# Order of the projection's side work and start of the recurrent stage in a fused two-block kernel

## The chip, the cores and the metric

The kernel runs on one core of a Trainium2 chip. The metric is the device time of one execution in microseconds; for the kernel before it is 2198.66 us, the median of three runs (2197.02 to 2201.4). TensorE is called PE, VectorE DVE, ScalarE ACT, GpSimd POOL and SyncE SP, as in the profile.

## The reference, cut to what matters

Two blocks work on one sequence of 512 tokens of width 1024. The first block normalises the tokens, projects them, and feeds 3072 of the projected columns (queries, keys, values; 8 heads of 128 each) through a convolution over 5 tokens and SiLU. Queries and keys are then scaled to unit length, and a gated delta rule runs over the tokens in both directions. The rest (a dilated attention, gates, a feed-forward part, and a second block of two hybrid layers) is not touched here.

```python
qkv = conv_over_5_tokens(proj[..., C_QA:C_ZA], conv_w)
qkv = jax.nn.silu(qkv)
qa = _l2norm(q heads) * (GDN_HEAD_DIM ** -0.5)
ka = _l2norm(k heads)
g_f = _gdn_decay(...)            # log-decay of each token and head
o_a = (_chunk_gated_delta(qa, ka, va, g_f, beta_f)
       + flip(_chunk_gated_delta(flip(qa), flip(ka), flip(va), flip(g_b), flip(beta_b))))
# recurrence: S_t = exp(g_t)(I - b_t k_t k_t^T) S_{t-1} + b_t k_t v_t^T,  o_t = S_t^T q_t
```

## The kernel before, in words

Every engine has its own program, written by hand; a helper notes for each instruction the semaphore value that it reaches, and the others wait for labels. An engine runs its program strictly in order. Results of PE go to one of 8 PSUM banks, which `job` (L365) hands out in rotation: a job waits until the job eight before it has been freed by its reader.

The **projection stage** ("qkv") makes 24 tiles of 128 columns by 512 tokens, numbered n and called (c, i): c from 0 to 5 (0, 1 queries, 2, 3 keys, 4, 5 values), i from 0 to 3. For each tile:

- PE multiplies it out, 24 matmuls (`fm`, L384, recorded on L396).
- ACT copies it from its bank (L831, here "the copy"). After the copies of i = 1 and 3 it also rounds a later piece of weights into its high part (`ahead`, L354), from which POOL makes the low part (L2152); both are 128x2048. It then finishes the tile before: SiLU (L819) once the convolution is done, and for c below 4 the square (L824).
- DVE convolves it: one operation on L863 and four on L866, all 128x512. Two buffers hold the copies and two the convolved tiles, so that the copy of tile n waits for the convolution of n-2.

Once in each c from 1 to 4 there is a **round of scaling** for c-1: PE sums the squares of its four tiles (`sums`, L763), ACT makes four reciprocal roots (`rsq`: four Ln, L800, then four Exp, L804), and DVE multiplies the four tiles by them (`scale_tiles`, L885). PE and ACT do this at i = 1, DVE at i = 2, after the convolution of that tile. Keys and values are also turned to token-major by PE (`turn`, L771) and copied out by ACT (`trans`, L810); values turn from a buffer of four tiles, which c = 5 writes again.

The log-decays are summed once: `gates_sum_pe` (L650) needs the label "g" of DVE (L724); ACT's `decays_act` and DVE's `gates_sums` and `gates_scales` go with it.

The **recurrent stage** ("gdn") works on four groups (direction, half of the heads), with 4 steps of 20 phases each, lagging by 0, 1, 8 and 9 slots:

```python
        PHASES = 20
        LAG = (0, 1, 8, 9)
        def in_flight():
            for slot in range(TT * PHASES + max(LAG)):
                for gi, (d, hf) in enumerate(groups):
                    if 0 <= slot - LAG[gi] < TT * PHASES:
                        s, ph = divmod(slot - LAG[gi], PHASES)
```

Phase 0 is PE's spread of the decays and ACT's shift (L996), phase 1 POOL's mask (L1035), phase 2 ACT's Exp (L1000), phase 3 the products qk and kk (L940) and DVE's two steps (L1073, L1076), phase 4 PE's transpose (L948) and DVE's first inverse (L1083, L1086); levels of matmuls follow. The values are first read in phase 17. `stage("gdn")` makes each of the four engines wait until PE, ACT and DVE have all ended the projection stage.

Of the kernel before, what the change touches and what calls it, by code (L numbers as in the profile page):

```python
# [15 lines left out]
ALU = mybir.AluOpType  # L16
ACT = mybir.ActivationFunctionType
# [152 lines left out]
def build(nc, xT, cols, base, gdnc, tabs, wgate, relb, sel, small, wts, out, scratch, old):  # L170
# [6 lines left out]
    with ctx:  # L177
# [553 lines left out]
        def gates_sums(dve, V):  # L731
            dve.wait_ge(*at(("pe", "gc")))
            V.tensor_copy(GCUM, ps("gc")[:, 0:64].rearrange("p (t c) -> p t c", c=16)).then_inc(*dve.did())
            V.tensor_copy(SM[5], ps("gc")[:, 64:128].rearrange("p (t c) -> p t c", c=16)).then_inc(*dve.did("gcc", free="gc"))
            dve.wait_ge(*dve.last())
            V.tensor_tensor(SM[4], SM[5], GCUM, ALU.subtract).then_inc(*dve.did("kd"))
            V.tensor_scalar(NEGC, GCUM, -1.0, None, ALU.mult).then_inc(*dve.did())

        def gates_scales(dve, V):
            dve.wait_ge(*at("eg"))  # L740
# [13 lines left out]
        def qkv_pe():  # L754
            pe = q["pe"]
            pe.stage("qkv", barrier=False)

            def sums(c):
                for i in range(4):
                    n = ("ss", c, i)  # L760
                    b = job(n)
                    pe.wait_ge(*at(("sq", c, i)))
                    pe.eng.matmul(b[:, :], ones, SQ2[:, i, :], start=True, stop=True).then_inc(*pe.did(("pe", n)))  # L763

            def turn(c):
                for i in range(4):
                    n = ("tr", c, i)
                    b = job(n)
                    pe.wait_ge(*at(("ktile", c, i) if c < 4 else ("vtile", c, i)))
                    for t in range(TT):  # L770
                        mm = pe.eng.transpose(b[:, t * P:(t + 1) * P], dst_tile(c, i)[:, t * P:(t + 1) * P], ident)  # L771
                    mm.then_inc(*pe.did(("pe", n)))

            for c in range(6):
                for i in range(4):
                    fm(("qkv", c, i), f"A{c}", i * P, HTS)
                    if c == 0 and i == 1:
                        gates_turn_pe()
                    if c == 1 and i == 0:
                        gates_sum_pe()  # L780
                    if 1 <= c <= 4 and i == 1:
                        sums(c - 1)
                    if c == 4 and i == 2:
                        turn(2)
                    if c == 5 and i == 0:
                        turn(3)
                    if c == 5 and i == 1:
                        turn(4)
            turn(5)

        def qkv_act():
            act = q["act"]
            act.stage("qkv")

            def rsq(c):
                for i in range(4):
                    act.wait_ge(*at(("pe", ("ss", c, i))))
                    if c:
                        act.wait_ge(*at(("scaled", c - 1, i)))
                    act.eng.activation(RS2[:, i, :], ps(("ss", c, i))[:, :], ACT.Ln, bias=col("eps"))\  # L800
                        .then_inc(*act.did(free=("ss", c, i)))
                act.wait_ge(*act.last())
                for i in range(4):
                    act.eng.activation(RS2[:, i, :], RS2[:, i, :], ACT.Exp, scale=-0.5).then_inc(*act.did(("rs", c, i)))  # L804

            def trans(c):
                dst = KTOK if c < 4 else VTOK
                for i in range(4):
                    act.wait_ge(*at(("pe", ("tr", c, i))))
                    act.eng.activation(dst[:, :, (c % 2) * 4 + i, :], ps(("tr", c, i))[:, :].rearrange("p (t c) -> p t c", c=P),  # L810
                                       ACT.Copy).then_inc(*act.did(free=("tr", c, i)))

            def finish(n):

                c, i = tiles[n]
                act.wait_ge(*at(("conv", n)))
                if c == 5:
                    act.wait_ge(*at(("pe", ("tr", 4, i))))
                act.eng.activation(dst_tile(c, i), CV[:, n % 2, :], ACT.Silu).then_inc(*act.did(("si", c, i), *([("vtile", c, i)] if c >= 4 else [])))  # L819
                if c < 4:  # L820
                    act.wait_ge(*act.last())
                    if c:
                        act.wait_ge(*at(("pe", ("ss", c - 1, i))))
                    act.eng.activation(SQ2[:, i, :], dst_tile(c, i), ACT.Square).then_inc(*act.did(("sq", c, i)))  # L824

            for n, (c, i) in enumerate(tiles):
                act.wait_ge(*at(("pe", ("qkv", c, i))))
                act.wait_ge(*at("xpzero"))
                if n >= 2:
                    act.wait_ge(*at(("conv", n - 2)))  # L830
                act.eng.activation(XP[:, n % 2, 2:S + 2], ps(("qkv", c, i))[:, :], ACT.Copy)\  # L831
                    .then_inc(*act.did(("xp", n), free=("qkv", c, i)))
                if i % 2:
                    ahead(f"A{c}", (i - 1) * P)
                if n:
                    finish(n - 1)
                if n == 1:
                    gates_act()
                if n == 5:
                    decays_act()  # L840
                if i == 1 and 1 <= c <= 4:
                    rsq(c - 1)
                if c == 4 and i == 3:
                    trans(2)
                if c == 5 and i == 0:
                    trans(3)
            finish(len(tiles) - 1)
            trans(4)
            trans(5)

        def qkv_dve():
            dve = q["dve"]
# [4 lines left out]
            for n, (c, i) in enumerate(tiles):  # L857
                dve.wait_ge(*at(("xp", n)))
                if n >= 2:
                    dve.wait_ge(*at(("si", *tiles[n - 2])))  # L860
                wc = lambda j: col("conv", (c * 4 + i) * CONV + j)
                cv = CV[:, n % 2, :]
                V.tensor_scalar(cv, XP[:, n % 2, 0:S], wc(0), None, ALU.mult).then_inc(*dve.did())  # L863
                for j in range(1, CONV):
                    dve.wait_ge(*dve.last())
                    V.scalar_tensor_tensor(out=cv, in0=XP[:, n % 2, j:j + S], scalar=wc(j), in1=cv, op0=ALU.mult,  # L866
                                           op1=ALU.add).then_inc(*dve.did(*([("conv", n)] if j == CONV - 1 else [])))
                if n == 1:
                    gates_biased(dve, V)
                elif n == 2:  # L870
                    gates_decay(dve, V)
                elif n == 4:
                    gates_sums(dve, V)
                elif n == 5:
                    gates_scales(dve, V)
                if 1 <= c <= 4 and i == 2:
                    scale_tiles(c - 1)

        def scale_tiles(c):
# [42 lines left out]

            return (ph - 5) // 2 + 1, (ph - 5) % 2

        def gdn_pe():
            pe = q["pe"]
            E = pe.eng
            pe.stage("gdn")

            def four(nm, s, gi, product, n=P, labels=()):  # L930

# [5 lines left out]
            for s, ph, gi, d, hf, c, k0 in in_flight():  # L937
# [3 lines left out]
                if ph == 0:  # L941
                    four("gr", s, gi, lambda o, h: mul(o, Gg[:, c, k0 + h:k0 + h + 1].broadcast_to([P, P]), tri(d)))
                elif ph == 3:
                    four("qk", s, gi, lambda o, h: mul(o, KF[:, 4 * hf + h, tok], QF[:, 4 * hf + h, tok]))
                    four("kk", s, gi, lambda o, h: mul(o, KF[:, 4 * hf + h, tok], KF[:, 4 * hf + h, tok]))
                elif ph == 4:
                    pe.wait_ge(*at(("abar", s, gi)))
                    four("p0", s, gi, lambda o, h: E.transpose(o, g[A_][:, h, :], ident))  # L948
# [21 lines left out]
                elif ph == 17:  # L970
                    if s:
                        pe.wait_ge(*at(("r", s, gi)))
                    pe.wait_ge(*at(("t", s, gi, 6)))
                    four("x", s, gi, lambda o, h: mul(o, g[U_][:, h, :], g[T_][:, h, :] if s else VTOK[:, c, 4 * hf + h, :]))
                elif ph == 19:
                    if s < TT - 1:
# [4 lines left out]
                    if s:  # L981
                        four("qs", s, gi, lambda o, h: mul(o, QF[:, 4 * hf + h, tok], ST[:, gi, h, :]))

        def gdn_act():
            act = q["act"]
            A = act.eng
            act.stage("gdn")
            for s, ph, gi, d, hf, c, k0 in in_flight():
                g = WRKG[gi]
                if ph == 0:  # L990
# [7 lines left out]
                elif ph == 2:  # L998
                    act.wait_ge(*at(("ddm", s, gi)))
                    A.activation(g[A_], g[A_], ACT.Exp).then_inc(*act.did(("gam", s, gi)))  # L1000
                elif ph in LEVELS and level(ph)[0] > 1 and not level(ph)[1]:

                    l = level(ph)[0] - 1
# [1080 lines left out]
        def _(eng):  # L2084
            q["pe"] = Queue(eng, "pe")
            load_pe()
            qkv_pe()
            gdn_pe()
            zg_pe()
            dil_pe()  # L2090
            merge_pe()
# [11 lines left out]
        def _(eng):  # L2103
            q["act"] = act = Queue(eng, "act")
            load_act()
            qkv_act()
            gdn_act()
            zg_act()
            dil_act()
            merge_act()  # L2110
# [170 lines left out]
```

## Time and profile before

| | |
|---|---|
| median of 3 runs | 2198.66 us |
| profiled execution, its own time | 2193.11 us |
| its span, first to last instruction | 2191.3 us |
| mean granted PE clock | 0.973 |
| busy share: PE / DVE / ACT / POOL | 95% / 45% / 34% / 28% |
| projection stage on PE | 35.75 to 209.5 us |
| recurrent stage on PE, first matmul | 211.03 us |

The span lies 1.8 us below the time of the same execution, and that time 5.6 us below the median of the runs. "Idle before" in a row is the time the engine stood still before the row, with what released it. Bars in a timeline merge like instructions that follow each other; the count stands after x.

### The profile page before, as it was taken

To read this page: it belongs to the slowest core of one execution; us is meant where nothing else is said; L and a number is where in the kernel's file an instruction comes from. 1 tells how busy PE (TensorE), PEld (TensorE's weight loads), DVE (VectorE), ACT (ScalarE), POOL (GpSimd) and SP (SyncE) were. 2 spreads that over 40 slices of the span, in tenths; PEclk is the share of its full clock that TensorE was granted. 3 is DMA by queue.
4 is the path that set the end of the run, shared out by engine and by line. 5 is a ranking of instruction groups with operands and counts; after the bars stand their busy time and mean duration, and the time that the engine had idled before them with its cause. 6 is when DMAs were issued, how large, how long until landed. Compare 5 with 4: busy or idle time off the path is not lost.

```text
span 2191.3 us, 27107 instructions
## 1 busy us (share of the span) xinstructions
PE 2082.2 (95%) x11564; PEld 1723.9 (79%) x11564; DVE 990.3 (45%) x1805; ACT 749.2 (34%) x1231; POOL 614.3 (28%) x206
## 2 busy tenths in 40 slices
PE   6998999999999999999889999988999999999998
PEld 3777999999977877787768888876686778776676
DVE  4895556565412222122376025133527753624762
ACT  4675132221533233222332122223324433334441
POOL 2331222133323223244325444422420004321001
PEclk9999899999999999999989999999999999999998
DMA  4221000000342233222212222222220003211001
GB/s 164 71 83 39 1 1 2 1 1 1 132 151 84 85 105 102 74 99 97 77 58 96 96 96 96 96 78 107 75 75 3 1 20 108 77 58 39 1 1 39
DMA packets 29009, 142.12 MB, mean 65 GB/s; under 512 B 2871, under 2 KB 7351, under 8 KB 14808
## 3 DMA queue, kind: packets, MB, share of 16 engines
q1 hardware_dynamic: 18944, 123.27, 15.8%
q10 hardware_dynamic: 9944, 17.12, 2.3%
q8 instruction: 91, 1.49, 0.3%
q14 instruction: 30, 0.25, 0.0%
HBM read 135.13 MB, written 5.24 MB: 64 GB/s over the span
## 4 chain that ended last, share of the span: by engine, by line
PE 88%; DVE 6%; ACT 4%; issue 1%; POOL 1%; DMA 0%; SPq 0%; POOLq 0%; DVEq 0%; ACTq 0%
PE bank L396 44%; PE bank L940 12%; PE bank L407 7%; PE bank L1778 5%; PE bank L1796 4%; PE bank L1785 3%; PE bank L597 2%; DVE WK L866 2%; PE bank L955 2%; PE bank L1273 1%; DVE WK L885 1%; ACT w_part L354 1%; PE bank L1249 1%; PE bank L1725 1%; PE bank L1243 1%
## 5 line engine op out<-in xcount | busy, mean ns | idle before, releaser
L396 PE MATMUL bank<-x_part,w_part 128*128 128x512 f32 x2976 | 699.3, 395 | 21.3 <-POOL w_part L2152 18.3
L396 PEld LDWEIGHTS bank<-x_part,w_part 128*128 128x128 f32 x2976 | 562.6, 190 | 143.7 <-POOL w_part L2152 18.7
L2152 POOL TENSOR_TENSOR w_part<-RAW,w_part 128x2048 fp32r<-128x2048 f32 (+1 forms) x90 | 402.9, 4480 | 815.3 <-ACT w_part L354 815.3
L940 PE MATMUL bank<-WK 128*128 128x64 f32 (+1 forms) x2336 | 281.1, 277 | 3.5 <-DVE WK L1086 1.7
L940 PEld LDWEIGHTS bank<-WK 128*128 128x128 f32 x2336 | 275.8, 196 | 4.3 <-DVE WK L1086 1.9
L2152 POOL TENSOR_TENSOR w_part<-WK,w_part 128x2048 fp32r<-128x2048 f32 (+1 forms) x30 | 126.2, 4205 | 386.0 <-ACT w_part L354 386.0
L354 ACT ACTIVATE w_part<-RAW 128x2048 fp32r<-128x2048 f32 (+1 forms) x90 | 166.3, 1849 | 179.4 <-PE bank L396 138.3
L396 PE MATMUL bank<-f_part,w_part 128*128 128x512 f32 x768 | 174.4, 389 | 0.0
L396 PEld LDWEIGHTS bank<-f_part,w_part 128*128 128x128 f32 x768 | 144.2, 188 | 29.9
L407 PE MATMUL bank<-w_part,x_part 128*128 128x256 f32 x1344 | 164.4, 284 | 0.0
L407 PEld LDWEIGHTS bank<-w_part,x_part 128*128 128x128 f32 x1344 | 162.1, 192 | 2.1 <-issue 1.5
L1778 PE MATMUL bank<-WK 64*128 64x512 f32 (+3 forms) x256 | 129.0, 589 | 5.5 <-ACT WK L1873 5.5
L1796 PE MATMUL bank<-WK 128*128 128x64 f32 x880 | 112.4, 268 | 0.0
L1796 PEld LDWEIGHTS bank<-WK 128*128 128x128 f32 x880 | 108.3, 192 | 0.2
L1785 PEld LDWEIGHTS bank<-BASE,WK 128*128 128x128 f32 x440 | 48.5, 142 | 71.5 <-issue 47.7
L866 DVE SCALAR_TENSOR_TENSOR WK<-WK,COL 128x512 f32<-128x512 f32 x96 | 101.8, 1060 | 3.4
L1007 ACT ACTIVATE WK<-bank 128x256 f32<-128x256 f32 x80 | 31.0, 387 | 199.4 <-PE bank L955 199.1
L396 PE MATMUL bank<-mix_part,w_part 128*128 128x512 f32 x384 | 87.6, 390 | 0.0
L396 PEld LDWEIGHTS bank<-mix_part,w_part 128*128 128x128 f32 x384 | 71.9, 188 | 14.9
L1430 DVE SCALAR_TENSOR_TENSOR WK<-bank,WK 128x512 f32<-128x512 f32 x16 | 11.1, 692 | 151.4 <-PE bank L1249 105.7
L1888 ACT ACTIVATE WK<-bank,WK 128x512 f32<-128x512 f32 x80 | 54.9, 686 | 65.2 <-DVE WK L2011 34.7
L2004 DVE TENSOR_REDUCE WK<-bank 128x1 f32<-128x512 f32 x80 | 54.8, 684 | 45.3 <-PE bank L1778 45.2
(253 smaller groups left out, 2413.5 us busy)
## 6 DMA issues: line engine op xcount, KB each, us to landing
RAW<-wts SPq DMA_DIRECT2D x84, 1024.0 KB, 4.8
WK<-wts SPq DMA_DIRECT2D x24, 1024.0 KB, 4.8
WK<-scratch ACTq DMA_DIRECT2D x16, 256.0 KB, 2.7
RAW<-wts SPq DMA_DIRECT2D x6, 512.0 KB, 3.5
WK<-wts SPq DMA_DIRECT2D x6, 512.0 KB, 3.5
scratch<-WK ACTq DMA_DIRECT2D x4, 768.0 KB, 3.3
WK<-xT SPq DMA_DIRECT2D x4, 512.0 KB, 5.7
WK<-xT ACTq DMA_DIRECT2D x1, 2048.0 KB, 11.3
```

The source lines that it names most:

```text
L354: act.eng.activation(high_part(i), raw_part(i), ACT.Copy).then_inc(*act.did(("hi", i)))
L396: mm = pe.eng.matmul(b[:, :], W[w][:, k, c:c + P], src[x][k], start=start and k == 0 and n == 0, stop=stop and k == kn - 1 and n == 2)
L407: mm = pe.eng.matmul(bank[:, lo:lo + n], src[x](k), W[w][:, k, c:c + n], start=k == 0 and j == 0, stop=k == KO - 1 and j == 2)
L597: mm = pe.eng.matmul(b[:, :], W[w][:, k, c:c + P], src[x][k], start=k == 0 and n == 0, stop=k == len(src[0]) - 1 and n == 2)
L866: V.scalar_tensor_tensor(out=cv, in0=XP[:, n % 2, j:j + S], scalar=wc(j), in1=cv, op0=ALU.mult, op1=ALU.add).then_inc(*dve.did(*([("conv", ...
L940: mul = lambda o, a, b: E.matmul(o, a, b, start=True, stop=True)
L1778: E.matmul(b[:, 0:len(ks) * P], qf[:, t * P:(t + 1) * P], kf[:, ks[0] * P:(ks[-1] + 1) * P], start=True, stop=True)\
L1785: mm = E.transpose(tb[:, j * P:(j + 1) * P], LGP[:, t, j * P:(j + 1) * P], ident)
L1796: mm = E.matmul(ob[:, t * 64:(t + 1) * 64], PTB[:, t % 2, j * P:(j + 1) * P], VT2[:, k, vc:vc + 64], start=j == 0, stop=j == len(ks) - 1)
L1888: A.activation(LGP[:, t, 0:w], src, ACT.Exp, bias=LST[:, 8 * (n % 2) + 4 + t:8 * (n % 2) + 5 + t], scale=sc, accum_out=LST[:, 16 + 4 * (n ...
L2004: V.tensor_reduce(mx, src, AX, ALU.max).then_inc(*dve.did(**({} if kind == "B" else dict(free=(L, "l", n, t)))))
L2152: eng.tensor_tensor(low_part(i), raw_part(i), high_part(i).bitcast(F32), ALU.subtract).then_inc(w_split, 1)
```

## The change

Three things move. The sums of the decays go from after tile (1, 0) to after tile (1, 2) on PE, and from n = 4, 5 to n = 6, 7 on DVE and from n = 5 to n = 7 on ACT. The round of scaling goes one tile later on all three engines (PE and ACT from i = 1 to 2, DVE from i = 2 to 3), and the turns of c = 3 and 4 follow. And PE and ACT no longer wait for the end of the projection stage: PE turns only tiles (5, 0) and (5, 1) before the recurrent stage, and (5, 2) and (5, 3) after the first group's qk and kk; ACT does the last SiLU and the copies of c = 5 after the first group's Exp. DVE and POOL keep their wait, and the first reader of the values waits for the last copy.

```diff
@@ -734,7 +734,7 @@
             V.tensor_copy(SM[5], ps("gc")[:, 64:128].rearrange("p (t c) -> p t c", c=16)).then_inc(*dve.did("gcc", free="gc"))
             dve.wait_ge(*dve.last())
             V.tensor_tensor(SM[4], SM[5], GCUM, ALU.subtract).then_inc(*dve.did("kd"))
-            V.tensor_scalar(NEGC, GCUM, -1.0, None, ALU.mult).then_inc(*dve.did())
+            V.tensor_scalar(NEGC, GCUM, -1.0, None, ALU.mult).then_inc(*dve.did("negc"))
 
         def gates_scales(dve, V):
             dve.wait_ge(*at("eg"))
@@ -762,8 +762,8 @@
                     pe.wait_ge(*at(("sq", c, i)))
                     pe.eng.matmul(b[:, :], ones, SQ2[:, i, :], start=True, stop=True).then_inc(*pe.did(("pe", n)))
 
-            def turn(c):
-                for i in range(4):
+            def turn(c, only=None):
+                for i in range(4) if only is None else (only,):
                     n = ("tr", c, i)
                     b = job(n)
                     pe.wait_ge(*at(("ktile", c, i) if c < 4 else ("vtile", c, i)))
@@ -776,17 +776,19 @@
                     fm(("qkv", c, i), f"A{c}", i * P, HTS)
                     if c == 0 and i == 1:
                         gates_turn_pe()
-                    if c == 1 and i == 0:
+                    if c == 1 and i == 2:
                         gates_sum_pe()
-                    if 1 <= c <= 4 and i == 1:
+                    if 1 <= c <= 4 and i == 2:
                         sums(c - 1)
                     if c == 4 and i == 2:
                         turn(2)
-                    if c == 5 and i == 0:
+                    if c == 5 and i == 1:
                         turn(3)
-                    if c == 5 and i == 1:
+                    if c == 5 and i == 2:
                         turn(4)
-            turn(5)
+            turn(5, 0)
+            turn(5, 1)
+            return turn
 
         def qkv_act():
             act = q["act"]
@@ -808,7 +810,7 @@
                 for i in range(4):
                     act.wait_ge(*at(("pe", ("tr", c, i))))
                     act.eng.activation(dst[:, :, (c % 2) * 4 + i, :], ps(("tr", c, i))[:, :].rearrange("p (t c) -> p t c", c=P),
-                                       ACT.Copy).then_inc(*act.did(free=("tr", c, i)))
+                                       ACT.Copy).then_inc(*act.did(("turned", c, i), free=("tr", c, i)))
 
             def finish(n):
 
@@ -836,17 +838,17 @@
                     finish(n - 1)
                 if n == 1:
                     gates_act()
-                if n == 5:
+                if n == 7:
                     decays_act()
-                if i == 1 and 1 <= c <= 4:
+                if i == 2 and 1 <= c <= 4:
                     rsq(c - 1)
                 if c == 4 and i == 3:
                     trans(2)
-                if c == 5 and i == 0:
+                if c == 5 and i == 1:
                     trans(3)
-            finish(len(tiles) - 1)
-            trans(4)
-            trans(5)
+                if c == 5 and i == 3:
+                    trans(4)
+            return finish, trans
 
         def qkv_dve():
             dve = q["dve"]
@@ -869,11 +871,11 @@
                     gates_biased(dve, V)
                 elif n == 2:
                     gates_decay(dve, V)
-                elif n == 4:
+                elif n == 6:
                     gates_sums(dve, V)
-                elif n == 5:
+                elif n == 7:
                     gates_scales(dve, V)
-                if 1 <= c <= 4 and i == 2:
+                if 1 <= c <= 4 and i == 3:
                     scale_tiles(c - 1)
 
         def scale_tiles(c):
@@ -922,10 +924,10 @@
 
             return (ph - 5) // 2 + 1, (ph - 5) % 2
 
-        def gdn_pe():
+        def gdn_pe(turn):
             pe = q["pe"]
             E = pe.eng
-            pe.stage("gdn")
+            pe.stage("gdn", barrier=False)
 
             def four(nm, s, gi, product, n=P, labels=()):
 
@@ -941,8 +943,14 @@
                 if ph == 0:
                     four("gr", s, gi, lambda o, h: mul(o, Gg[:, c, k0 + h:k0 + h + 1].broadcast_to([P, P]), tri(d)))
                 elif ph == 3:
+                    if s == 0 and gi == 0:
+                        for i in range(4):
+                            pe.wait_ge(*at(("scaled", 3, i)))
                     four("qk", s, gi, lambda o, h: mul(o, KF[:, 4 * hf + h, tok], QF[:, 4 * hf + h, tok]))
                     four("kk", s, gi, lambda o, h: mul(o, KF[:, 4 * hf + h, tok], KF[:, 4 * hf + h, tok]))
+                    if s == 0 and gi == 0:
+                        turn(5, 2)
+                        turn(5, 3)
                 elif ph == 4:
                     pe.wait_ge(*at(("abar", s, gi)))
                     four("p0", s, gi, lambda o, h: E.transpose(o, g[A_][:, h, :], ident))
@@ -971,6 +979,7 @@
                     if s:
                         pe.wait_ge(*at(("r", s, gi)))
                     pe.wait_ge(*at(("t", s, gi, 6)))
+                    pe.wait_ge(*at(("turned", 5, 3)))
                     four("x", s, gi, lambda o, h: mul(o, g[U_][:, h, :], g[T_][:, h, :] if s else VTOK[:, c, 4 * hf + h, :]))
                 elif ph == 19:
                     if s < TT - 1:
@@ -981,10 +990,11 @@
                     if s:
                         four("qs", s, gi, lambda o, h: mul(o, QF[:, 4 * hf + h, tok], ST[:, gi, h, :]))
 
-        def gdn_act():
+        def gdn_act(finish, trans):
             act = q["act"]
             A = act.eng
-            act.stage("gdn")
+            act.stage("gdn", barrier=False)
+            act.wait_ge(*at("negc"))
             for s, ph, gi, d, hf, c, k0 in in_flight():
                 g = WRKG[gi]
                 if ph == 0:
@@ -998,6 +1008,9 @@
                 elif ph == 2:
                     act.wait_ge(*at(("ddm", s, gi)))
                     A.activation(g[A_], g[A_], ACT.Exp).then_inc(*act.did(("gam", s, gi)))
+                    if s == 0 and gi == 0:
+                        finish(len(tiles) - 1)
+                        trans(5)
                 elif ph in LEVELS and level(ph)[0] > 1 and not level(ph)[1]:
 
                     l = level(ph)[0] - 1
@@ -2084,8 +2097,7 @@
         def _(eng):
             q["pe"] = Queue(eng, "pe")
             load_pe()
-            qkv_pe()
-            gdn_pe()
+            gdn_pe(qkv_pe())
             zg_pe()
             dil_pe()
             merge_pe()
@@ -2103,8 +2115,7 @@
         def _(eng):
             q["act"] = act = Queue(eng, "act")
             load_act()
-            qkv_act()
-            gdn_act()
+            gdn_act(*qkv_act())
             zg_act()
             dil_act()
             merge_act()
```

## Rows read from the trace of the kernel before

**Rows 1.** the page, part 4: shares of the chain that ended last, by engine

```profile
PE 88%; DVE 6%; ACT 4%; issue 1%; POOL 1%; DMA 0%; SPq 0%; POOLq 0%; DVEq 0%; ACTq 0%
```

**Rows 2.** windows: length, busy PE PEld DVE ACT POOL, clock, DMA, GB/s

```profile
136.00:163.00 27.00, 25.54 (x105) 19.50 (x105) 25.09 (x26) 19.39 (x27) 9.69 (x2) 1.00 0.24 85
```

**Rows 3.** timeline of PE, projection stage: start, length, row, idle before

```profile
68.47 1.02 PE L658 MATMUL bank<-STAT,WK 128*128 128x8 f32 x4 [4.69 <-DVE STAT L724]
...
73.61 7.41 PE L396 MATMUL bank<-x_part,w_part 128*128 128x512 f32 x24
...
162.95 1.12 PE L763 MATMUL bank<-WK,BASE 128*128 128x512 f32 x2 [1.16 <-ACT WK L824]
...
171.06 11.14 PE L396 MATMUL bank<-x_part,w_part 128*128 128x512 f32 x48
...
201.90 1.03 PE L771 MATMUL bank<-BASE,WK 128*128 128x128 f32 x8
...
207.56 1.97 PE L771 MATMUL bank<-BASE,WK 128*128 128x128 f32 x8 [4.63 <-ACT WK L810]
```

**Rows 4.** timeline of DVE, projection stage

```profile
82.21 7.33 DVE L866 SCALAR_TENSOR_TENSOR WK<-WK,COL 128x512 f32<-128x512 f32 x4
...
124.46 6.91 DVE L885 SCALAR_TENSOR_TENSOR WK<-WK 128x512 f32<-128x512 f32 x4
...
131.29 0.47 DVE L863 TENSOR_SCALAR WK<-WK,COL 128x512 f32<-128x512 f32 x1
...
134.84 0.48 DVE L863 TENSOR_SCALAR WK<-WK,COL 128x512 f32<-128x512 f32 x1
...
138.90 7.36 DVE L866 SCALAR_TENSOR_TENSOR WK<-WK,COL 128x512 f32<-128x512 f32 x4
...
147.56 0.49 DVE L863 TENSOR_SCALAR WK<-WK,COL 128x512 f32<-128x512 f32 x1 [1.30 <-ACT WK L831]
...
177.11 2.49 DVE L885 SCALAR_TENSOR_TENSOR WK<-WK 128x512 f32<-128x512 f32 x4
...
203.25 3.12 DVE L866 SCALAR_TENSOR_TENSOR WK<-WK,COL 128x512 f32<-128x512 f32 x4
```

**Rows 5.** timeline of ACT, one round of scaling and what stands around it

```profile
136.63 1.91 ACT L354 ACTIVATE w_part<-RAW 128x2048 fp32r<-128x2048 f32 x1
...
138.50 0.63 ACT L819 ACTIVATE WK<-WK 128x512 f32<-128x512 f32 x1
...
139.81 1.28 ACT L800 ACT_TABLE_LOAD   x1
...
141.11 2.42 ACT L800 ACTIVATE WK<-bank,COL 128x512 f32<-128x512 f32 x4
...
146.94 0.58 ACT L831 ACTIVATE WK<-bank 128x512 f32<-128x512 f32 x1
```

**Rows 6.** timeline of POOL, the low part of a weight piece

```profile
138.62 4.73 POOL L2152 TENSOR_TENSOR w_part<-RAW,w_part 128x2048 fp32r<-128x2048 f32 x1 [7.79 <-ACT w_part L354]
```

**Rows 7.** timeline of all engines, start of the recurrent stage

```profile
206.93 4.00 ACT L810 ACTIVATE WK<-bank 128x512 f32<-128x512 f32 x8
...
214.48 1.27 POOL L1035 TENSOR_TENSOR WK<-WK 128x512 f32<-128x512 f32 x1 [44.51 <-ACT WK L996]
...
215.98 1.28 ACT L1000 ACT_TABLE_LOAD   x1
...
218.13 0.69 DVE L1073 TENSOR_TENSOR WK<-bank,WK 128x512 f32<-128x512 f32 x1 [11.77 <-ACT WK L1000]
...
223.15 0.68 DVE L1073 TENSOR_TENSOR WK<-bank,WK 128x512 f32<-128x512 f32 x1
...
228.65 1.11 PE L940 MATMUL bank<-WK 128*128 128x64 f32 x8 [1.74 <-DVE WK L1086]
```

**Rows 8.** windows, columns as in rows 2: the clock around two stretches

```profile
66.00:68.00 2.00, 0.00 (x0) 0.00 (x0) 1.93 (x4) 1.97 (x4) 0.00 (x0) 0.74 0.00 0
...
231.40:241.60 10.20, 10.20 (x52) 10.20 (x52) 1.81 (x5) 1.81 (x6) 1.26 (x1) 0.53 0.01 2
```

## The prediction, made before the changed kernel was run

> **What bounds the kernel now.** I read the chain of waits first: 88% of the time lies on PE [rows 1], so a gap on PE looks like time to be had. The timeline of PE shows the gaps that this change aims at: 4.69 us ahead of the sums of the decays, a wait of 1.16 us at the last square of a round of scaling (the longest of three such), and 4.63 us inside the last turn, followed by 1.5 us until 211.03 [rows 3]. The question is then what PE waits for. One round, 27 us, has PE busy 25.54 us and DVE 25.09 us [rows 2]: two engines are nearly full, and the third, ACT, passes work between them. So the timelines of DVE and ACT over one round come next, and they show a closed chain that is longer than PE's work:
>
> - DVE takes 3.55 us to convolve a tile (131.29 to 134.84), and four scalings take 2.49 us where POOL is idle [rows 4].
> - While POOL makes a low part (138.62 to 143.35, [rows 6]), DVE's operation on two SBUF tensors stands still: four of them take 7.36 us where they otherwise take 3.12, and the four scalings 6.91 us in place of 2.49 [rows 4]. One low part that falls on DVE costs it 4.3 us, and there are two in a round.
> - ACT's part runs from the end of a convolution (138.38, where the next tile's first operation ended its 3.55 us after 134.84) over SiLU and square, to 139.81, the four Ln and four Exp, to 146.94, and the next copy, to 147.56, where DVE goes on [rows 4, 5]: 9.2 us.
>
> The chain of one round is: convolution 3.55, scaling with a low part on it 6.83, two convolutions 7.1, ACT 9.2: 26.7 us. PE's tiles take 5.55 us each (171.06: two in 11.14, [rows 3]) and it has a gap in every round, so PE follows the chain. Under ACT's 9.2 us DVE does one convolution with the other low part on it, 7.87 us (138.38 to 146.26), and idles only the 1.30 us of the row at 147.56 [rows 4]. **That low part is hidden under the roots; this is what the change disturbs.**
>
> **The change, part by part.**
>
> **1. Sums of the decays later.** PE's wait of 4.69 us goes, and so does its slow start: the clock had fallen in that gap (0.74 of full in the window 66 to 68, [rows 8]) and 24 matmuls at 73.61 took 7.41 us where they otherwise take 5.5 [rows 3]. PE gains some 8 us there. I cost it at nothing, because ACT and DVE are behind by then: DVE's convolution of tile (1, 1) runs to 89.46 with a low part on it [rows 4], and that depends on the queue of DVE, not on PE. The cover is this lag; if it were not there, these 8 us would count.
>
> **2. Squares one tile later.** The roots now stand between ACT's copies of tiles (c, 2) and (c, 3), and the scaling follows the convolution of (c, 3). Queued behind the roots on ACT are the copy of (c, 3), which DVE waits for, and the rounding of a weight piece, which POOL waits for. I go round the new chain:
>
> - copy of (c, 3) done, convolution of (c, 3). ACT's rounding follows the copy, POOL starts some 2.5 us after the copy began (0.58 and 1.91, [rows 5]) and so inside this convolution: 3.55 + 4.32 = 7.87 us.
> - scaling, free of POOL: 2.49 us.
> - convolution of (c+1, 0). ACT's copy of (c+1, 1) needs only the convolution of (c, 3), so its rounding is done about 3.8 us after that, and POOL meets this convolution: 7.87 us again.
> - convolution of (c+1, 1): 3.55 us.
> - ACT's 9.2 us, to the copy of (c+1, 3). DVE has one plain convolution to do meanwhile, 3.55 us, and idles 5.6 us.
>
> The sum is 31.0 us a round against 26.7: **4.3 us more, the low part that has come out of its cover.** In place of PE's small wait at the last square stand larger ones.
>
> From tile to tile: the convolution of (1, 1) ends at about 89.2. ACT's 9.2 us give 98.4 for the convolution of (1, 3), then two rounds of 31.0 give 160.4 for that of (3, 3). From there 7.87 + 2.49 + 7.87 + 3.55 = 21.8 us lead to 182.2, the end of the convolution of (4, 1). PE's tile (4, 3) needs the bank that the first Ln of the last round frees: SiLU 0.75 (no square for values), table load 1.28, one Ln 0.6, so 184.8. Before it started at 171.06 [rows 3]. From there PE is the slower one, as in the kernel before (30.84 us from 171.06 to 201.90 without a gap), so **+13.8 us** for the end of tile (5, 3).
>
> **3. Start of the recurrent stage.** POOL keeps its wait for DVE's end of the projection, so the head start is not the whole turn. Before, the last convolution ended at 206.37 [rows 4], eight copies and the last products followed, and DVE began the first group at 218.13 [rows 7]: 11.8 us. After: PE has the spread of the decays and ACT the shift done when the convolution ends (ACT is free of its four copies some 3.2 us after tile (5, 3)), POOL's mask takes 1.27, and from the mask's end to DVE it is 2.38 us (215.75 to 218.13, [rows 7]), with 0.1 for the handover 3.8 us. **Gain 8.0 us.**
>
> **4. What is now in the way of the second group.** Its Exp stands on ACT behind the last SiLU (with a table load), four copies at 0.5 (eight took 4.00) and a table load back. That is 2 x 1.28 + 0.63 + 2.1, with Exp's own 0.6 some 5.9 us after the first group reaches DVE, where 5.0 us were taken before (223.15 against 218.13, [rows 7]). The wait at 228.65 [rows 7], the last before PE is full, hangs on this group: **+0.9 us.** On PE the turn of (5, 3) waits for that SiLU, and the transpose of the first group stands behind it; it is held up by 0.4 us, less than the second group. The Trainium skill (ScalarE: Activation LUTs, What ACT_TABLE_LOAD costs) gives 2.66 us for a switch of tables, the drain included; the trace shows 1.29 us from load to Exp, and I keep that. By the page this term would be about 3.7 us.
>
> **5. PE's clock.** It was halved after each of the two gaps of over 4 us. The new kernel has such a gap ahead of tile (4, 3), where PE is the slower one afterwards. By the row at 73.61 against 5.5 that costs 1.9 us: **+1.9 us**, with nothing and 4 us as ends. At the start of the recurrent stage PE idles some 5 us, as before, and I take no change. Before, PE was full at 0.53 of the clock from 231.4 to 241.6 [rows 8]; at most half of these 10.2 us come back if the clock is full there, and a longer slow stretch would cost about 3.
>
> Sum: 13.8 - 8.0 + 0.9 + 1.9 = **+8.6 us**. The profiled execution takes 2193.11 us (span 2191.3 and 1.8 around it) and would take 2201.7. It lies 5.6 us under the median of the runs, so the same step from 2198.66 gives **2207.3 us**.
>
> **Rivals.**
>
> **A, faster: the low parts stay covered.** If POOL's operation fell under the roots, or DVE caught up between, the round would stay at 26.7 us or get 1 us shorter, the waits at the squares would be gone, and the head start would remain: -8.0 + 0.9 - 1 = -8.1 us, 2190.6 us. Against it: in every round of before, POOL starts 2 us after ACT's rounding begins, and ACT's order fixes that. The turning point is a growth of the projection by 7.1 us instead of 13.8, or a round longer by about 2 us instead of 4.3. Chance 0.14.
>
> **B, the slow clock moves.** The round grows as said, but the new stage begins so that its full stretch meets the full clock: 5.1 us less, 2202.2 us. For it: the slow stretch of before lay 13 us behind DVE's first step, and the phase of it is not fixed by the program. Chance 0.10.
>
> **C, the head start is empty.** The turn of (5, 3) and the copies hold up both groups, the recurrent stage starts as late after tile (5, 3) as before: 13.8 + 1.9 = +15.7 us, 2214.4 us. Against it: DVE's first step needs none of them. Chance 0.07.
>
> **How the numbers follow.** My forecast has 0.69, with its own ends 2204 to 2213.5: the price of a low part may be between 3.9 and 4.7 us (POOL's 4.73 less one step of DVE, and the whole of it), three times over, and the clock's ends. About 0.2%, 4.4 us, can be told from no change here; so slower is the forecast and C, 0.76; the same is B, 0.10; faster is A, 0.14. The range reaches from 2198 us, under B with a cheaper low part, to 2215 us over C; outside it are A and what lies above.
>
> **What would show it.** Right: DVE waits of about 5.5 us for the copy (L831) four times between 90 and 192 us, instead of 1.3; both low parts of a round on convolutions and four scalings at 2.5 us; PE waits of over 4 us at L763 from c = 3 on, and one ahead of tile (4, 3) at about 185; tile (5, 3) ends near 216 to 219; DVE's first step (L1073) 3.8 us after the last convolution. No wait ahead of L658. Wrong: rounds of 27 us or less, or a last convolution before 210; then A holds. If L1073 comes over 8 us after the last convolution, C.

## The result, and the profile after

| | before | changed |
|---|---|---|
| median of 16 runs | 2197.93 us | 2206.2 us |
| ratio, 95% interval | | 1.0034 (1.002 to 1.0047) |
| profiled span | 2191.3 us | 2204.8 us |

The change makes the kernel slower, by 8.3 us between the medians; the interval of the ratio puts the loss between 4.4 and 10.3 us.

A round is the stretch of DVE from one convolution that had to wait for ACT's roots to the next. In the kernel before, it runs from the row below to that at 147.56 in [rows 4] and takes 26.65 us (timeline of DVE, kernel before):

```profile
120.91 0.49 DVE L863 TENSOR_SCALAR WK<-WK,COL 128x512 f32<-128x512 f32 x1 [1.32 <-ACT WK L831]
```

The same in the changed kernel, from the convolution of one tile (c, 3) to the next (timeline of DVE):

```profile
129.07 0.49 DVE L865 TENSOR_SCALAR WK<-WK,COL 128x512 f32<-128x512 f32 x1 [5.55 <-ACT WK L833]
129.59 7.24 DVE L868 SCALAR_TENSOR_TENSOR WK<-WK,COL 128x512 f32<-128x512 f32 x4
136.75 2.49 DVE L887 SCALAR_TENSOR_TENSOR WK<-WK 128x512 f32<-128x512 f32 x4
...
139.68 7.33 DVE L868 SCALAR_TENSOR_TENSOR WK<-WK,COL 128x512 f32<-128x512 f32 x4
...
159.65 0.49 DVE L865 TENSOR_SCALAR WK<-WK,COL 128x512 f32<-128x512 f32 x1 [5.54 <-ACT WK L833]
```

From 129.07 to 159.65 it is 30.58 us, 3.9 us more. The four scalings are short now (2.49 against 6.91 us), and two convolutions of the round are long (7.24 and 7.33 us). POOL's two low parts lie on just these two, and neither lies beside the roots any longer (timeline of POOL):

```profile
130.92 4.58 POOL L2163 TENSOR_TENSOR w_part<-RAW,w_part 128x2048 fp32r<-128x2048 f32 x1 [15.82 <-ACT w_part L354]
140.52 5.15 POOL L2163 TENSOR_TENSOR w_part<-RAW,w_part 128x2048 fp32r<-128x2048 f32 x1 [5.03 <-ACT w_part L354]
```

While ACT loads the table for the roots and computes them (151.91 to 159.12 in its timeline), DVE finishes one plain convolution and then idles 5.54 us, in place of the 1.30 us of [rows 4]. The timeline of PE answers to [rows 3]:

```profile
75.55 0.51 PE L658 MATMUL bank<-STAT,WK 128*128 128x8 f32 x4
...
138.21 1.90 PE L763 MATMUL bank<-WK,BASE 128*128 128x512 f32 x2 [3.53 <-ACT WK L826]
...
178.71 1.11 PE L771 MATMUL bank<-BASE,WK 128*128 128x128 f32 x4 [5.79 <-ACT WK L833]
183.77 19.37 PE L396 MATMUL bank<-x_part,w_part 128*128 128x512 f32 x72 [3.94 <-ACT WK L802]
202.98 1.91 PE L771 MATMUL bank<-BASE,WK 128*128 128x128 f32 x16
...
218.14 1.04 PE L771 MATMUL bank<-BASE,WK 128*128 128x128 f32 x8
```

The wait of 4.69 us for the decays is gone, but PE now waits up to 3.5 us at the squares, 5.8 us inside a turn (for a bank) and 3.9 us ahead of tile (4, 3), which starts at 183.77 where it was 171.06. The turn behind tile (5, 3) begins at 218.14 where it was 201.90, 16.2 us later. The granted clock had fallen in those gaps; over this stretch it was 0.68 of full (windows, columns as in rows 2):

```profile
163.00:190.00 27.00, 13.82 (x39) 9.22 (x38) 21.14 (x21) 13.94 (x20) 8.14 (x2) 0.68 0.00 1
```

The start of the recurrent stage (timeline of all engines) answers to [rows 7]:

```profile
219.50 3.11 DVE L868 SCALAR_TENSOR_TENSOR WK<-WK,COL 128x512 f32<-128x512 f32 x4
...
222.85 2.48 POOL L1048 TENSOR_TENSOR WK<-WK 128x512 f32<-128x512 f32 x2 [46.68 <-ACT WK L1006]
223.49 1.28 ACT L1010 ACT_TABLE_LOAD   x1
...
225.63 0.69 DVE L1086 TENSOR_TENSOR WK<-bank,WK 128x512 f32<-128x512 f32 x1 [3.02 <-ACT WK L1010]
...
227.40 1.11 PE L771 MATMUL bank<-BASE,WK 128*128 128x128 f32 x4 [4.02 <-ACT WK L821]
...
231.27 0.69 DVE L1086 TENSOR_TENSOR WK<-bank,WK 128x512 f32<-128x512 f32 x1 [0.45 <-ACT WK L1010]
...
236.42 1.11 PE L942 MATMUL bank<-WK 128*128 128x64 f32 x8 [1.74 <-DVE WK L1099]
```

DVE begins the first group 3.0 us after the end of the last convolution (222.61), where it took 11.8; the head start is real. The last wait before PE is full comes at 236.42 against 228.65: +7.8 us. Of these, 1.1 us arose before the projection's rounds: DVE's first step on the gates, L713, came at 60.88 against 59.83, ahead of everything that the change moves. The other 5.7 of the 13.5 us between the two spans lie later. From the first matmul on L407 to that on L1262 (L1249 before) it took 100.5 us against 95.9, with the granted clock lower in it (in the kernel before it was 1.00 throughout):

```profile
608.00:628.00 20.00, 20.00 (x65) 13.95 (x64) 0.00 (x0) 5.60 (x11) 2.36 (x1) 0.83 0.45 170
```

In the single profiles of the experiments the same stretch took 95.9 to 100.6 us: 99.0 once without the head start (e1) and 95.9 once with it (e5), though most profiles with the head start have the longer time. One profile of each kernel cannot say how often it occurs, so this stretch is no evidence on the change either way. Of the comparison of spans 4.6 us stay open by it, and the medians are the better measure.

### The profile page after: what moved, and what is told of

It reads as the page before. It is cut to its first block, busy times and chain, and to the rows that moved or that the text cites. A ratio compares the mean times of both kernels' runs of the same rounds, so it can differ in the third digit from the quotient of the medians.

```text
span 2204.8 us, 27117 instructions
## 1 busy us (share of the span) xinstructions
PE 2087.4 (95%) x11564; PEld 1724.9 (78%) x11564; DVE 985.8 (45%) x1805; ACT 752.8 (34%) x1234; POOL 615.0 (28%) x206
## 3 DMA queue, kind: packets, MB, share of 16 engines
q1 hardware_dynamic: 18944, 123.27, 15.7%
## 4 chain that ended last, share of the span: by engine, by line
PE 87%; DVE 8%; ACT 4%; issue 1%; POOL 1%; DMA 0%; SPq 0%; POOLq 0%; DVEq 0%; ACTq 0%
PE bank L396 44%; PE bank L942 12%; PE bank L407 7%; PE bank L1791 5%; PE bank L1809 4%; DVE WK L868 4%; PE bank L1798 3%; PE bank L597 2%; PE bank L963 2%; PE bank L1286 1%; PE bank L1262 1%; PE bank L1738 1%; ACT w_part L354 1%; PE bank L1256 1%; PE bank L1825 0%
## 5 line engine op out<-in xcount | busy, mean ns | idle before, releaser
L396 PE MATMUL bank<-x_part,w_part 128*128 128x512 f32 x2976 | 705.4, 398 | 25.2 <-POOL w_part L2163 18.3
L407 PE MATMUL bank<-w_part,x_part 128*128 128x256 f32 x1344 | 164.4, 284 | 0.0
L407 PEld LDWEIGHTS bank<-w_part,x_part 128*128 128x128 f32 x1344 | 162.1, 191 | 2.1 <-issue 1.5
L868 DVE SCALAR_TENSOR_TENSOR WK<-WK,COL 128x512 f32<-128x512 f32 x96 | 114.2, 1190 | 3.4
L396 PEld LDWEIGHTS bank<-mix_part,w_part 128*128 128x128 f32 x384 | 71.9, 188 | 14.9
```

Source lines behind the costliest of these rows:

```text
L396: mm = pe.eng.matmul(b[:, :], W[w][:, k, c:c + P], src[x][k], start=start and k == 0 and n == 0, stop=stop and k == kn - 1 and n == 2)
L407: mm = pe.eng.matmul(bank[:, lo:lo + n], src[x](k), W[w][:, k, c:c + n], start=k == 0 and j == 0, stop=k == KO - 1 and j == 2)
```

## The experiments

The theory is that of the prediction: the later round of scaling takes a low part out from under the roots, and DVE pays 4.3 us for it in each round. The rivals are that the loss sits in the start of the recurrent stage, or that the later round is dear by its order, whatever POOL does. Each table gives the median of the experiment and then that of the kernel before on the same chip.

### One part alone

```diff
# e1_squares: the kernel before, with
-                    if 1 <= c <= 4 and i == 1:
+                    if 1 <= c <= 4 and i == 2:
                         sums(c - 1)
...
# and so rsq at i == 2, scale_tiles at i == 3, turn(3), trans(3), turn(4) one tile later
```

> The kernel before with the round of scaling one tile later, and nothing else of the change. Theory (a low part has come out from under the roots, 4.3 us a round): the last convolution of the projection ends 14 to 17 us later than in the kernel before, and with no head start all of that shows: 15 us slower, about 2213. DVE waits of 5.5 us for the copy in each round. Rival (the loss of the changed kernel sits in the start of the recurrent stage, where turns and copies stand in the way): the time of the kernel before, within 2 us, or a little less because the waits of PE at the squares go.

```diff
# e2_decays: the kernel before, with
-                    if c == 1 and i == 0:
+                    if c == 1 and i == 2:
                         gates_sum_pe()
...
# and decays_act, gates_sums, gates_scales at n = 7, 6, 7
```

> The kernel before with the sums of the decays later, and nothing else. Theory (ACT and DVE set the pace of the projection): PE's wait of 4.7 us goes and turns up as waits of PE later; the time stays within 2 us of the kernel before, the last convolution ends at most 2 us earlier. Rival (gaps of PE count): 8 us faster, about 2190.

```diff
# e3_head: the kernel before, with
-            turn(5)
+            turn(5, 0)
+            turn(5, 1)
+            return turn
...
# and the parts of the change in gdn_pe, gdn_act and the end of qkv_act
```

> The kernel before with the head start of the recurrent stage alone: PE and ACT do not wait, two value tiles are turned later; decays and squares as before. Theory: last convolution to DVE's first step of the recurrent stage takes 3 to 4 us in place of 11.8; 7 to 9 us faster, about 2190. Rival (the second group gives back what the first gains): within 3 us of the kernel before.

| part alone | median, kernel before | ratio, 95% interval |
|---|---|---|
| squares later | 2215.4, 2198.36 us | 1.0086 (1.0071 to 1.01) |
| decays later | 2195.84, 2198.36 us | 0.9992 (0.9981 to 1.0003) |
| head start | 2191.59, 2198.36 us | 0.9969 (0.9958 to 0.9979) |

By medians +17.0, -2.5 and -6.8 us, together +7.7 where the change gives +8.3: the parts add up within their intervals, which are some 6 us wide for the squares and for the change. The loss is in the squares alone, and the recurrent stage's start is a gain; the first rival is out. The interval of the decays alone holds 1, so their -2.5 us are not shown. With the squares alone, DVE waits as in the changed kernel:

```profile
131.90 0.49 DVE L863 TENSOR_SCALAR WK<-WK,COL 128x512 f32<-128x512 f32 x1 [5.55 <-ACT WK L831]
...
162.58 0.49 DVE L863 TENSOR_SCALAR WK<-WK,COL 128x512 f32<-128x512 f32 x1 [5.54 <-ACT WK L831]
```

With the decays alone, PE's wait of 4.69 us was replaced by one of 6.44 us for a square: PE only came sooner to the next thing it has to wait for (timeline of PE):

```profile
79.25 2.05 PE L763 MATMUL bank<-WK,BASE 128*128 128x512 f32 x2 [6.44 <-ACT WK L824]
```

### The same order, with the low part back under the roots

```diff
# e5_cover: the changed kernel, with, in qkv_act
-                if i % 2:
-                    ahead(f"A{c}", (i - 1) * P)
+                if i >= 2:
+                    ahead(f"A{c}", (i - 2) * 2 * P)
```

> The changed kernel, but ACT rounds the weight piece of i = 1 one tile later (after the copy of tile (c, 2)), so that POOL makes the low part while the roots are computed, as in the kernel before. Squares as late as in the changed kernel. Theory: the rounds fall from 30.6 to about 26.7 us, DVE has no 5.5 us waits, the last convolution is back at 205 to 207 plus the start's scatter, and the head start remains: about 2190, 15 us less than the changed kernel. Rival (a later round of scaling is dear by its order, whatever POOL does): stays within 3 us of 2206.

2188.47 against 2198.36 us, ratio 0.9963 (0.9949 to 0.9978): in each c one rounding by ACT, moved by one tile, turns the loss into a gain of 9.9 us. The squares stand as late as in the changed kernel, so the order is not what costs. A low part now lies on the convolution that runs beside the roots, and the round is 26.5 us (123.72 to 150.19; timelines of DVE and, last, of POOL):

```profile
123.72 0.49 DVE L865 TENSOR_SCALAR WK<-WK,COL 128x512 f32<-128x512 f32 x1 [1.34 <-ACT WK L833]
124.25 7.35 DVE L868 SCALAR_TENSOR_TENSOR WK<-WK,COL 128x512 f32<-128x512 f32 x4
131.51 2.49 DVE L887 SCALAR_TENSOR_TENSOR WK<-WK 128x512 f32<-128x512 f32 x4
...
141.53 7.36 DVE L868 SCALAR_TENSOR_TENSOR WK<-WK,COL 128x512 f32<-128x512 f32 x4
150.19 0.49 DVE L865 TENSOR_SCALAR WK<-WK,COL 128x512 f32<-128x512 f32 x1 [1.30 <-ACT WK L833]
...
141.25 4.74 POOL L2163 TENSOR_TENSOR w_part<-RAW,w_part 128x2048 fp32r<-128x2048 f32 x1 [10.99 <-ACT w_part L354]
```

The edit also moves the rounding in c = 0, ahead of the rounds. That explains little: the convolution of (1, 3) starts 1.4 us sooner than in the changed kernel (96.94 against 98.30), the last convolution 14.9 us sooner (204.11 against 218.98).

### POOL that writes and does not read

```diff
# e6_before_fill (the kernel before) and e7_after_fill (the changed one), for pieces 2 to 11
-                eng.tensor_tensor(low_part(i), raw_part(i), high_part(i).bitcast(F32), ALU.subtract).then_inc(w_split, 1)
+                eng.memset(low_part(i).bitcast(F32), 0.0).then_inc(w_split, 1)
```

> The kernel before, but for the weight pieces 2 to 11 of the projection POOL only fills the low part with zeros and reads nothing from SBUF (so the low parts of these weights are left out of the products; all matmuls still run). Theory: an operation of POOL that reads nothing holds up DVE's operations on two tensors no longer, scalings and convolutions take 2.5 and 3.6 us throughout, PE sets the pace at about 25.2 us a round: the last convolution ends 8 to 11 us earlier, about 2188. Rival (DVE is slow for another reason than POOL's reads): within 3 us of the kernel before.

> The changed kernel with the same replacement as e6 (low parts of weight pieces 2 to 11 filled with zeros, not computed). Theory: with no low part to come out of its cover, the later round of scaling costs nothing, and the change is a gain: 8 to 10 us below e6, about 2179, last convolution at 192 to 197. Rival (the later round costs by its order, or by PE's clock): about 8 us above e6, as the change is above the kernel before.

2183.09 and 2178.67 us, against 2199.38 us for the kernel before: ratios 0.9932 (0.9911 to 0.9952) and 0.9907 (0.9882 to 0.9932). Both lie below the kernel before, and the sign of the change is turned: -4.4 us where it was +8.3, with all four runs of e7 below all four of e6. DVE's operations on two tensors are short now, in groups by line, first e6 from 64 to 200 us, then the kernel before from 64 to 210 us:

```profile
L866 DVE SCALAR_TENSOR_TENSOR WK<-WK,COL 128x512 f32<-128x512 f32 x84 | 63.2, 752 | 3.0
L885 DVE SCALAR_TENSOR_TENSOR WK<-WK 128x512 f32<-128x512 f32 x16 | 10.0, 685 | 0.0
```

```profile
L866 DVE SCALAR_TENSOR_TENSOR WK<-WK,COL 128x512 f32<-128x512 f32 x88 | 87.3, 992 | 3.1
L885 DVE SCALAR_TENSOR_TENSOR WK<-WK 128x512 f32<-128x512 f32 x16 | 23.2, 1514 | 0.0
```

Of the eight fills in that stretch of e6, five lie on convolutions and three on scalings, and none of these is longer for it, as here (timelines of DVE and POOL):

```profile
100.07 3.11 DVE L866 SCALAR_TENSOR_TENSOR WK<-WK,COL 128x512 f32<-128x512 f32 x4
...
100.39 1.81 POOL L2153 MEMSET w_part<- 128x2048 f32 x1 [7.73 <-ACT w_part L354]
```

The expected 8 to 10 us between the two kernels were a miss, and so was 2188 us for e6, which came out 5 us lower. In the profiles the head start is worth its 8.7 us in e7 (3.04 us to DVE's first step, where e6 has 11.77), but the last convolution begins at 193.06 against 190.41. PE was full in both, and in e7 its granted clock was 0.82 and 0.75 in the two stretches of 4 us from 76 on, where e6 had 1.00; a wait of 0.39 us for a bank in the turns comes to it. With no lag of DVE to hide them, both count. The fill also takes only 1.8 us where the subtraction took 4.7, so these two runs show that POOL's subtraction is the cause; they do not tell its reading from its length.

### Better than both

```diff
# e4_decays_head: the changed kernel with sums, rsq, scale_tiles and the turns at their old i
# e8_both_covered: e4, with
-                if i % 2:
-                    ahead(f"A{c}", (i - 1) * P)
+                if i == 1:
+                    ahead(f"A{c}", 0)
# e9_both_nodecays: e8 with the decays at their old place
# e10_second_first: e8, with, in gdn_pe and in gdn_act
-                    if s == 0 and gi == 0:
+                    if s == 0 and gi == 1:
```

> The changed kernel with the round of scaling put back to i = 1 and 2 as before: decays later and head start. Theory: the gains of the two alone, 2 and 7 us, add up, about 2189. Rival (the three parts need each other): above 2195.

> As e4, and ACT rounds both weight pieces of a chunk together after the copy of tile (c, 1), ahead of the roots, so that POOL makes both low parts while DVE has nothing else to wait for. Theory: scalings take 2.5 us, the round falls from 26.7 to about 25.3 us (DVE's own work and PE's, nearly equal), the last convolution ends 6 to 9 us earlier than in e4: about 2181. Rival (two low parts on one convolution of 12 us outlast the roots, and ACT waits in turn): 2189, no better than e4.

> As e8 (both low parts made under the roots, head start, squares as before), with the sums of the decays back at their old place. In e8 DVE has 25.3 us of work a round and PE 25.2, so PE's wait is now close to the path. Theory: the decays' old place costs again PE's wait of 4.7 us and its slow clock, but DVE is the slower one until tile (1, 1) is convolved; last convolution 0 to 3 us later than in e8, time 2180 to 2184. Rival (once the low parts are covered PE alone sets the pace): 8 us above e8, 2188.

> As e8, but ACT does the last SiLU and the copies of c = 5, and PE the turns of (5, 2) and (5, 3), only after the second group's Exp and its qk and kk. Theory (term 4 of the prediction): the second group reaches DVE 5.0 us after the first in place of 5.6, PE's wait of 3.1 us ahead of the turn of (5, 3) shrinks; 0.5 to 1.5 us less than e8, too little for the comparison of times, to be read in the trace. Rival (copies come too late and hold up banks of the second group's kk): second group later than 5.6 us after the first, time above e8.

| | median, kernel before | ratio, 95% interval |
|---|---|---|
| e4 | 2186.14, 2199.38 us | 0.9945 (0.993 to 0.996) |
| e8 | 2180.43, 2199.38 us | 0.9921 (0.9899 to 0.9943) |
| e9 | 2186.06, 2198.62 us | 0.9941 (0.9924 to 0.9958) |
| e10 | 2177.14, 2198.62 us | 0.9900 (0.9885 to 0.9916) |

In e8 both low parts lie on one convolution, 11.60 us long, beside the roots. DVE does not idle, and the round is 25.2 us (118.67 to 143.88). That is DVE's own work, and also PE's, which has no gap in it either (126.99 to 152.21, from one set of squares to the next):

```profile
118.67 2.49 DVE L887 SCALAR_TENSOR_TENSOR WK<-WK 128x512 f32<-128x512 f32 x4
...
128.69 11.60 DVE L868 SCALAR_TENSOR_TENSOR WK<-WK,COL 128x512 f32<-128x512 f32 x4
...
143.88 2.49 DVE L887 SCALAR_TENSOR_TENSOR WK<-WK 128x512 f32<-128x512 f32 x4
```

In e9 the old place of the decays cost 5.6 us by the medians (4.4 by the two ratios), more than the 0 to 3 expected and less than the rival's 8. With DVE's lag gone, PE's wait of 4.70 us ahead of L658 counts: the convolution of (1, 1) starts at 83.08 where it was 76.7 in e8, and the last one at 200.14 against 194.44, 5.7 us later. e10 has the lowest median. The second group reaches DVE 5.0 us after the first (201.22, 206.25) as expected, but the median lies 3.3 us below that of e8, more than expected. The four runs of each overlap (2173.07 to 2178.89 and 2178.14 to 2183.72 us), so this gain is not shown beyond doubt; what the profiles say of it is in the last section.

## Why the prediction was right

**2207.3 us were forecast and 2206.2 measured**, with 2198 to 2215 as the range. Point by point:

- Step 1, decays at nothing: by itself -2.5 us, with an interval of the ratio that holds 1. Right, and for the reason given: e9 shows the same part worth 4 to 6 us once the cover is gone. It was not quite nothing in the trace: with the gates' operations out of the way, DVE began the convolution of (1, 1) at 81.36 against 81.69, although it had started 1.1 us later.
- Step 2, a round of 31.0 us: 30.6. The copy of (1, 3) led to a convolution at 98.30 (98.4 forecast), tile (4, 3) started at 183.77 (184.8). The first agreement is in part luck: the late start of 1.1 us and the 1.4 us that DVE won back by the decays cancelled. e5 shows that the exposed low part is the cause, not the order.
- Step 3, 3.8 us from the last convolution to DVE: 3.0, a gain of 8.7 us for 8.0. The table load for Exp began at 223.49, before the mask of the first group was done (the row at 222.85 holds two masks, 2.48 us together); in the kernel before it came after that mask, and I had counted it so.
- Step 4, +0.9 us: the second group came 5.64 us after the first, where it was 5.02: +0.6. By the Trainium skill's price for a switch of tables (ScalarE: Activation LUTs, What ACT_TABLE_LOAD costs, 2.66 us) an estimate of this term would be 3.7 us. The trace does not agree: from the table load at 223.49 to Exp it is again 1.29 us.
- Step 5, +1.9 us for the clock: the three tiles from 183.77 took 19.2 us (to 202.98) where 3 x 5.55 would be 16.65: 2.6. The turns behind them took 0.7 us more, 0.4 of it a wait for a bank at 212.06 that the forecast did not have. The recurrent stage had its slow stretch in both kernels, as assumed: the granted clock was 0.50 from 232 to 240 us before and from 238 to 246 after, with PE full.
- Sum at the last wait of the recurrent stage's start: +7.8 us, of which 1.1 is not the change's, so 6.7 for 8.6. The projection came out at 15.1 (16.2 less 1.1) for 15.7, and the steps 3 and 4 were too dear by 0.7 and 0.3. The medians moved by 8.3; that this lies within 0.3 of the forecast is in part luck, as the interval of the ratio is 6 us wide and the trace accounts for 6.7.
- Rivals: A's condition (a growth of the projection below 7.1 us) was not met, 16.2. B's clock did not come back here, but it did in e10. C is excluded by the 3.0 us.
- Signs: DVE's waits for the copy were 4.91, 5.55, 5.54 and 8.32 us, with the scalings at 2.49, and nothing stands ahead of L658. One sign failed: the waits at L763 were to be over 4 us from c = 3 on and were 3.53 and 3.45. The longest wait of PE, 5.79 us for a bank inside the turn of c = 2, was not among the signs.

That POOL's operation stops DVE's two-tensor ones was taken from the trace. The Trainium skill (SBUF — State Buffer, Who interferes with whom) has it as a rule: a DVE instruction with two SBUF inputs contends with a GpSimd instruction that reads SBUF, and not with one that only writes. The runs agree on both: 7.3 us for four such operations with the low part on them, and in e6 a mean of 752 ns for the 84 in a stretch with eight fills.

## What to carry to other kernels

Before moving work to close a gap on the busiest engine, ask what that engine would wait for next, and what lies under the step that is moved: here DVE's wait for ACT was the cover for an operation of POOL that stops DVE, and moving that wait by one tile without moving ACT's rounding, which starts POOL, uncovered it. Such an operation belongs beside a stretch in which DVE has to wait anyway; put there on purpose, both low parts together gave 5.7 us (e8 against e4).

## What the runs showed of the hardware beyond that

POOL's fill did not touch DVE's operations on two tensors, but it did hold up the one-tensor operation that starts a convolution. Each of the three that began during a fill in e6 ended 0.3 us after the fill did, and took 1.06, 1.60 and 1.60 us where it takes 0.48 (e6, timelines of POOL and DVE; this fill ends at 116.55, the operation at 116.84):

```profile
114.74 1.81 POOL L2153 MEMSET w_part<- 128x2048 f32 x1 [12.54 <-ACT w_part L354]
...
115.24 1.60 DVE L863 TENSOR_SCALAR WK<-WK,COL 128x512 f32<-128x512 f32 x1
```

In one pair of profiles the granted clock at the start of the recurrent stage was worth more than the waits themselves. With PE equally full, the same 12 us held 60 matmuls at half clock in e8 and 111 at full clock in e10 (windows, columns as in rows 2, first e8, then e10):

```profile
213.00:225.00 12.00, 12.00 (x60) 12.00 (x60) 2.12 (x5) 1.76 (x6) 0.00 (x0) 0.51 0.01 1
```

```profile
213.00:225.00 12.00, 12.00 (x111) 12.00 (x111) 3.81 (x9) 6.07 (x16) 2.53 (x2) 1.00 0.01 1
```

In the stretch before it, 201 to 213, PE was busy 8.10 us in e8 and 8.96 us in e10. The last wait before PE is full ends 0.5 us sooner in e10 (211.39 against 211.90), and the third group reaches DVE 6.7 us sooner (226.27 against 232.92); the spans differ by 6.7 us too (2175.2 and 2181.9). Whether e10 gets the full clock in every execution, one profile cannot tell; its median is 3.3 us below that of e8, from four runs each.
